# The pairs of the second mixer: 64x64 block products on all four quadrants of TensorE, in two token layouts

## The reference, cut to what matters

```python
def step(state, inp):
    r_t, w_t, k_t, v_t, kk_t, a_t = inp
    s_kk = jnp.einsum('bhij,bhj->bhi', state, kk_t)
    state = (state * w_t[:, :, None, :]
             - s_kk[..., None] * (kk_t * a_t)[:, :, None, :]
             + v_t[..., None] * k_t[:, :, None, :])
    return state, jnp.einsum('bhij,bhj->bhi', state, r_t)
```

## Time and profile before

| | us |
|---|---|
| median of 3 runs | 2676.55 |
| lowest and highest of the 3 | 2674.39, 2678.38 |
| span of the profiled execution | 2685.8 |
| PE busy in it | 2553.3 (95%) |
| DVE busy | 1283.3 (48%) |
| ACT busy | 678.3 (25%) |

### The profile page before, as it was taken

The page is one execution under the profiler, slowest core; times in us unless marked ns, Lnnn a source line. Parts: engine busy times, 40 slices in busy tenths (PEclk is TensorE's granted clock), DMA queues, the critical chain, the costliest instruction groups (busy, mean ns, idle before and its releaser), DMA issues. The chain is left out here.

```text
span 2685.8 us, 44310 instructions
## 1 busy us (share of the span) xinstructions
PE 2553.3 (95%) x17988; PEld 1728.1 (64%) x17988; DVE 1283.3 (48%) x2682; ACT 678.3 (25%) x1184; POOL 166.2 (6%) x128
## 2 busy tenths in 40 slices
PE   8999999999999899899998979999999999999997
PEld 3666666588875667566665636756787555677644
DVE  4656655667643222222222137524777335655525
ACT  2333333101112111111111111133454223343422
POOL 0000000000000022222222200000000000000000
PEclk9999999999999899999999989999999799999999
DMA  6222202335332789999999952441010232111120
GB/s 273 111 84 89 79 32 86 118 126 204 141 122 99 284 322 368 391 338 391 338 391 357 361 201 80 139 173 61 27 51 31 74 147 73 63 63 49 62 75 32
DMA packets 83737, 436.67 MB, mean 163 GB/s; under 512 B 16432, under 2 KB 16944, under 8 KB 39888
## 3 DMA queue, kind: packets, MB, share of 16 engines
q1 hardware_dynamic: 54592, 372.92, 35.3%
q0 software_dynamic: 18096, 37.80, 5.4%
q10 hardware_dynamic: 10848, 23.10, 2.3%
HBM read 400.65 MB, written 61.41 MB: 172 GB/s over the span
## 5 line engine op out<-in xcount | busy, mean ns | idle before, releaser
L284 PE MATMUL psum_all<-u,weights 128*128 128x512 f32 x704 | 306.9, 593 | 0.0
L284 PEld LDWEIGHTS psum_all<-u,weights 128*128 128x128 f32 x704 | 132.4, 190 | 157.7 <-issue 157.3
L964 PE MATMUL psum_all<-big,weights 128*128 128x256 f32 x928 | 214.7, 381 | 2.1 <-ACT sq L1021 1.3
L1898 PE MATMUL psum_all<-big 128*32 128x256 f32 (+2 forms) x1648 | 194.1, 382 | 8.1 <-DMA big<-t_experts 6.6
L1898 PE MATMUL psum_all<-weights,big 128*64 128x256 f32 (+2 forms) x1296 | 187.8, 388 | 10.2 <-DMA weights<-t_experts 9.5
L964 PEld LDWEIGHTS psum_all<-big,weights 128*128 128x128 f32 x928 | 174.5, 190 | 34.2 <-issue 5.1
L964 PE MATMUL psum_all<-big 128*128 128x256 f32 x784 | 179.0, 379 | 0.0
L1898 PEld LDWEIGHTS psum_all<-weights,big 128*64 128x64 f32 (+2 forms) x1296 | 131.9, 145 | 50.7 <-issue 16.1
L964 PEld LDWEIGHTS psum_all<-big 128*128 128x128 f32 x784 | 148.7, 190 | 22.4 <-DVE big L2617 0.8
L1898 PEld LDWEIGHTS psum_all<-big 128*32 128x32 f32 (+2 forms) x1648 | 136.0, 132 | 41.6 <-issue 10.0
L1933 DVE COPY big<-psum_all 128x256 f32<-128x256 f32 x46 | 19.5, 424 | 282.0 <-PE psum_all L294 282.0
(11 more groups left out here) (472 smaller groups left out, 3989.6 us busy)
## 6 DMA issues: line engine op xcount, KB each, us to landing
big<-t_experts SPq DMA_DIRECT2D x96, 1024.0 KB, 28.6
weights<-t_experts SPq DMA_DIRECT2D x96, 1024.0 KB, 26.7
weights<-t_ada SPq DMA_DIRECT2D x24, 1024.0 KB, 7.0
weights<-t_rkvg SPq DMA_DIRECT2D x16, 1024.0 KB, 8.6
rwkv_inputs<-big ACTq DMA_DIRECT2D x48, 256.0 KB, 2.3
big<-rwkv_inputs SPq DMA_DIRECT2D x8, 1280.0 KB, 6.8
weights<-t_x SPq DMA_DIRECT2D x8, 1024.0 KB, 4.8
weights<-t_BC SPq DMA_DIRECT2D x8, 1024.0 KB, 5.0
```

The lines of the kernel that those rows point to most:

```text
L284: last = pe.matmul(out, lhsT, rhs, start=n == 0, stop=n == len(terms) - 1)
L964: ins = pe.matmul(out, w[:, k, :], x[:, k, :], start=first and k == 0, stop=k == n - 1, skip_group_check=not first)
L1898: ins = pe.matmul(K.psum[rows, bank, n * F_E:(n + 1) * F_E], xT[:, k, rows], X.part(r, n, KD, F_E)[:, k, :], start=k == 0, stop=k == KD - 1)
```

## The change

Blocks get a new order, and there are two layouts of the tokens. `place(c, layout)` says for chunk c which partition half, which of two slots and which u it has; in layout 1 half and slot are exchanged. A set made by `turned_pe` reads one layout and writes the other: operands from half r, result in half `slot`, bank r of a unit. A unit is two banks (`K.unit` waits for the readers of both). Three sets (X0, X1, X2), each added to X on VectorE, go: the first inverse is now a product of A1, A2, A4 and A8, which are M and its powers with the identity added: P = A4·A1, Q = A2·P, X = A8·Q. P, Q and X are copied by ScalarE. Q alone stays in its layout (`straight_pe`, two quadrants).

```diff
-def blocks_pe(K, q, p, name, lhsT, rhs, reader):
-    for i in range(8):
-        for r in range(2):
-            ins = pe.matmul(K.psum[half(r), b, HEAD * i:HEAD * (i + 1)], lhsT[half(r), i, :], rhs[half(r), i, :],
+def place(c, layout):
+    u, tile_bit, half_bit = c // 4, c // 2 % 2, c % 2
+    return (tile_bit, half_bit, u) if layout == 0 else (half_bit, tile_bit, u)
+
+def turned_pe(K, q, p, name, lhsT, rhs, reader):
+    pe = K.nc.tensor
+    K.unit(UNIT[name], reader, name + " read", p)
+    for u in range(2):
+        for h in range(2):
+            for slot, r in ((0, 0), (1, 1), (1, 0), (0, 1)):
+                i = block(slot, u, h)
+                ins = pe.matmul(in_unit(K, name, half(slot), r, u, h), lhsT[half(r), i, :], rhs[half(r), i, :], start=True, stop=True)
+    ins.then_inc(*q.pe.tick(name, p))
@@ inside_pe: the same order of quadrants, first all four of qb, then all four of qk
@@ C1_pe: each of the 16 products of 64x128 becomes two of 64x64, one per layout
@@ turn_y_pe: 4 transposes become 4 matmuls by the identity
-    transposes(K, [(tile(K.psum[:, 7, :], t), X.yt[p % 2]...) for t in range(NT)])
+            ins = K.nc.tensor.matmul(out[:, u, slot], rows[:, slot, P * u:P * u + P], ident, start=True, stop=True)
@@ Q_pe, X_pe
+    K.nc.tensor.wait_ge(*q.dve.at("A2", p))
+    K.nc.tensor.wait_ge(*q.act.at("P read", p))
+    straight_pe(K, q, p, "Q", X.A2, X.N, q.act)
...
+    K.nc.tensor.wait_ge(*q.dve.at("NT3 read", p))
+    K.nc.tensor.wait_ge(*q.act.at("Q read", p))
+    turned_pe(K, q, p, "X", X.A8, X.NT, q.act)
@@ pair_pe: tv after to_state 1, bonus after to_state 2, NT, N, MT2 one place later
+    P_pe(K, X, q, s)
+    from_state_pe(K, X, q, s - 1, 6)
     NT3_pe(K, X, q, s)
-    from_state_pe(K, X, q, s - 1, 6)
-    tal_pe(K, X, q, s)
     to_state_pe(K, X, q, s - 1, 6)
     early.pe(s == KD, 1)
     tka_pe(K, X, q, s)
+    Q_pe(K, X, q, s)
     from_state_pe(K, X, q, s - 1, 7)
-    X2_pe(K, X, q, s)
+    X_pe(K, X, q, s)
@@ pair_act
+    P_act(K, X, q, s - 1)
     gain_act(K, X, q, s - 3)
     tka_act(K, X, q, s - 1)
     expp_act(K, X, q, s)
+    Q_act(K, X, q, s - 1)
+    X_act(K, X, q, s - 1)
     T16_act(K, X, q, s - 1)
@@ pair_dve: A2 for X0's add, A4 for X1's, A8 (two instructions) for X2's
     ends_dve(K, X, q, s - 1)
+    A4_dve(K, X, q, s - 1)
     S_dve(K, X, q, s - 2, 6)
-    add_X_dve(K, X, q, s - 1, "X1")
...
     normed_dve(K, X, q, s - 3)
+    A8_dve(K, X, q, s - 1)
     start_S_dve(K, X, q, s - 1)
-    add_X_dve(K, X, q, s - 1, "X2")
@@ al_dve and rh_dve: one 128x512 product becomes two of 128x256
+    for u in range(2):
+        ins = K.nc.vector.tensor_tensor(turned_chunks(X.alrh[p % 2], u, part_of), chunks(a, u), chunks(b, u), ALU.mult)
```

More of the change, by code:

```diff
@@ L267, in bank, with unit @@
         return self.psum[:, b, :]
+    def unit(self, n, signal, *key):
+        before = dict.fromkeys(self.held[b] for b in (2 * n, 2 * n + 1))
+        for earlier in before:
+            if earlier is not None:
+                s, k = earlier
+                self.nc.tensor.wait_ge(*s.at(*k))
+        self.held[2 * n] = self.held[2 * n + 1] = signal, key
 def load(K, i, view):
@@ L2719 @@
 SLOW = float(np.exp(-0.5))
[L2722 to L2726, removed]
+UNIT = {"y": 2, "T16": 0, "G16": 1, "A16": 1, "G32": 0, "T32": 1, "A32": 0, "TaT": 1, "Wv": 0, "C2": 1, "C1": 0, "MT": 1,
+        "WX": 0, "NT": 1, "N": 0, "MT2": 1, "M2": 0, "P": 1, "NT3": 0, "Q": 1, "X": 0}
+TOKENS_BANK = {"tv": 7, "tka": 7, "tal": 7, "tbe": 0}
 def outside(p):
@@ L2769, in channels_pe @@
[L2769 to L2777, removed]
-    ins.then_inc(*q.pe.tick(name, p))
+    half_of, slot, u = place(c, 0)
+    return X.alrh[p % 2][:, 2 * u + slot, :, HEAD * half_of:HEAD * (half_of + 1)]
@@ new lines, in straight_pe, with quarters @@
+def straight_pe(K, q, p, name, lhsT, rhs, reader):
+    pe = K.nc.tensor
+    K.unit(UNIT[name], reader, name + " read", p)
+    for slot in range(2):
+        for u in range(2):
+            for h in range(2):
+                i = block(slot, u, h)
+                for r in range(2):
+                    ins = pe.matmul(in_unit(K, name, half(r), slot, u, h), lhsT[half(r), i, :], rhs[half(r), i, :], start=True, stop=True)
+    ins.then_inc(*q.pe.tick(name, p))
+def quarters(layout):
+    for u in range(2):
+        for slot in range(2):
+            for r, h in ((0, 0), (1, 1), (0, 1), (1, 0)):
+                yield (4 * u + 2 * r + slot if layout == 0 else 4 * u + 2 * slot + r), h
@@ L2805, in tal_pe @@
     K.nc.tensor.wait_ge(*q.dve.at("al", p))
[L2806 to L2809, removed]
+    tokens_pe(K, q, p, "tal", lambda t: X.alrh[p % 2][:, t, 0, :])
 def C1_pe(K, X, q, p):
@@ L2983, in from_state_pe @@
         return
-    pe, rows = K.nc.tensor, half(c % 2)
+    pe, at = K.nc.tensor, P * (c % 2)
     if c == 0:
@@ L3038, in turn_y_pe @@
     K.bank(7, q.act, "yf", p)
-    transposes(K, [(tile(K.psum[:, 7, :], t), X.yt[p % 2].rearrange("p b n -> p (b n)")[:, t * P:(t + 1) * P]) for t in range(NT)]) \
-        .then_inc(*q.pe.tick("turn y", p))
+    rows = two_slots(X.yt[p % 2])
+    out = K.psum[:, 7, :].rearrange("p (u t r n) -> p u r t n", t=2, r=2, n=HEAD)
+    ident = K.c("ident").rearrange("p (t n) -> p t n", n=HEAD)
+    for u in range(2):
+        for slot in range(2):
+            ins = K.nc.tensor.matmul(out[:, u, slot], rows[:, slot, P * u:P * u + P], ident, start=True, stop=True)
+    ins.then_inc(*q.pe.tick("turn y", p))
 def mean_pe(K, X, q, p):
```

343 lines of the change are left out of this document (213 added, 130 removed).

## The result

The changed kernel takes 2729.15 us (median of 4 runs, 2724.57 to 2732.57) against 2675.47 us for the kernel before beside it (2673.17 to 2678.38): a ratio of 1.0189, with a 95% interval of 1.0162 to 1.0216. It is 53.7 us slower. The prediction, 2700.0 with a range of 2680 to 2722, has the direction and less than half of the size, and the measured time lies outside its range. The profiled execution has a span of 2725.7 us.

A forecast was written before the change was run, and what follows sets the result against it. VectorE was taken to bound the walk, a TensorE chain the tail. Per iteration -2.64 + 3.85 + 1.3 = +2.5, +2.3 with stalls, +4.1 with clock, times 6; with small terms +23.5, median 2676.55 to 2700, range 2680 to 2722.

The forecast's parts named there:

- the wait ahead of X: TensorE between from_state 7 and X: waiting for Q's copy behind gain, tka and Ep, 3.85 us more an iteration.
- the tail: From X to A32's adding: shorter sets on four quadrants, 10.74 us instead of 13.38, 2.64 less an iteration.
- the clock forecast at +1.8: TensorE right behind X: clock falls to 1.2 GHz at most waits, 1.8 us an iteration, from 0 to 2.6.
- the walk: Walk over the chunks: Al in halves, A4 and P, and Q ahead of from_state 7 add 1.3 us an iteration.
- I let half of it stay: Pairs' iterations: half the excess from stalls no engine's wait explains (mean 34.3 against 33.77) stays, making +2.5 into +2.3.
- the profile's 0.35% as a scale factor: Whole kernel: profiled execution lies 0.35% over the runs' median, so forecast 2709 for the profile becomes 2700 for the median.
- the last y gains about 1: Last y of the stage: about 1 us less.
- the first pairs: Pair 0: +1 us for one more level of product and copy; pair 1: -0.5 us, as X waits for A8 only.
- C: Rival: all as forecast, but the clock holds, +2.3 us in each of six iterations, 2690 us; chance 0.22.
- D: Rival: clock stays at 1.2 GHz for much of each iteration, some 8 us more each, 2725 us; chance 0.10.
- 21 us of work: TensorE in one iteration: claimed to work some 21 of 36 us, becoming 42 at 1.2 GHz.
- A: Rival: TensorE's work is what counts, 7.5 us less an iteration in full, 2617 us, or 2669; chance 0.12.

The follow-up runs named there:

- e5: Changed kernel with A4, A8, P and Q made earlier and gain behind X's copy on ScalarE: 2700.05 us, ratio 1.0085.
- e2: Changed kernel with four full-array matmuls that nothing reads filling TensorE's wait ahead of X: 2722.42 us, ratio 1.0151.
- e1: Kernel before, unedited, run and profiled once more: 2678.34 us, ratio 1.0001.
- e3: Changed kernel with one line moved, gain behind X's copy on ScalarE instead of ahead of tka's: 2718.22 us, ratio 1.0148.
- e10: Kernel of e5 with each turned set issuing 4 larger products instead of 16, output not the reference's: 2679.84 us, ratio 0.9999.
- e6: Changed kernel with matmuls that nothing reads ahead of X, P, TaT and to_state 0, in the last walk too: 2710.77 us, ratio 1.0138.
- e9: Changed kernel with each turned set issuing 4 larger products instead of 16, output not the reference's: 2719.22 us, ratio 1.0155.
- e7: Kernel before with two matmuls that nothing reads, ahead of TaT and to_state 0, in the last walk alone: 2676.79 us, ratio 1.0004.
- e8: Kernel of e5 with the two last-walk filling matmuls of e7 added: 2693.97 us, ratio 1.007.

## Why the prediction was off

**Right: the wait ahead of X.** 3.85 more was forecast, 4.13 behind from_state 7; measured are 4.32 in most iterations, 4.30 in the mean and 4.02 more than before, in the order gain, tka, Ep, Q. With the order that avoids it the kernel is 27 us faster by the excess (e5).

**Right: the tail.** 10.74 from X to A32's adding at full clock: 10.87 in the iteration of after that leads to pair 1, and in e2. With the clock forecast at +1.8, the tail's net is -0.84; measured is 12.85 against 13.81, -0.96. The page rule of the Trainium skill that was weighed there, in "TensorE: Matmul & The Clock Gate", section "Wait — 56ns, not 53.3ns?", an interval of at least about 25 ns from start to start, does not hold for these records: 32 of them start within 0.51 us in after as well (2097.39 to 2097.90 in its timeline), 16 ns each.

**Right at full clock, wrong as a whole: the walk.** The step is "I take 1.3 more, with bounds -0.5 and +2". The undisturbed walk takes 21.33 (1896.00 in after, one in e2), which is 1.3 over the 20.0 of before. Whether by the parts that were added up isn't shown: e5 takes Q out of the walk's end but puts A8 in. The mean is 23.35, 3.3 over e1 (3.18 over the first profile), beyond the bound. Two terms that the walk's sum did not have fill the gap:
- The clock in the walk. The prediction let it fall behind the wait of X alone and priced 5 us of it there. Measured are 25.8 us at 1.2 GHz in the six walks together. The two worst walks (8.8 and 10.2 us of it) took 25.31 and 26.31, 4 to 5 us over the undisturbed one, and the six together lost about 8.5 us by it, an estimate, 1.4 an iteration. The earlier trace rows had shown, at 2106, that the clock falls in a walk with small groups and waits between, without a long gap. The prediction read it and used it for a rival only.
- The gaps of instruction supply. "I let half of it stay" was the step: fewer stalls of the kind of the earlier trace rows were to come. (That one too stands 1.3 us behind a packet's end; the profile names ScalarE's copy, which had ended 0.8 us before it.) The reverse is so. They rose from 2.2 or 3.4 us to 6.0 from 1896 to 2139, and in the six walks from 1.3 or 0.8 to 4.9, some 0.6 a walk. The more of the waits is removed or filled, the more of them appears: 8.7 in e3, 9.5 in e2, 17.4 in e5.

The sum, 1.3 + 1.4 + 0.6 = 3.3, is the walk's excess. The split between the two last terms is read from single walks and is rough.

**Wrong: the profile's 0.35% as a scale factor.** The profiled execution lay 9 us over the median, and the prediction carried that over as if it were spread evenly, from 2709 to 2700. It was one place: the last walk at 0.66, 12 us. With it went the last term, "the last y gains about 1": the forecast let this stretch gain 1 us, and in the changed kernel's profile, where it is slow too, the rest is 12.5 longer than in e1. This is the largest single miss. The kernel before pays it in some of its runs and, by their times, in none of the four beside the changed kernel. What was to be read was the clock row of the page and the earlier trace rows, whose third line is in that walk. This is the clock row of the first profile:

```profile
PEclk9999999999999899999999989999999799999999
```

Slice 32, from 2081.5 to 2148.6 us, is its only dip from the stage of the pairs on.

**The sum of the misses.** Against e1 the forecast missed 6 x 2.04 = 12.2 in the walks (23.35 - 20.01 - 1.3), 13.5 in the rest (12.5 measured, -1 forecast) and 2.7 in the first pairs (3.2 measured, 0.5 forecast). Another 1.1 is the wait and the tail of the six iterations (37.9 measured, 24.6 forecast, less the 12.2). With the 23.5 of the forecast that is 53.0, against 53.6 between the spans and 53.7 between the medians. What makes up the 3.2 of the first pairs is not known.

**The rivals.** C (the clock holds) is out by the windows. D (the clock down much of each iteration, 2725, given 0.10) came nearest in time, with the wrong size at the wrong place: the clock is down for 64.9 us of the 243 of the six iterations, not in most of each. (No row gives its "21 us of work"; the profile has TensorE busy 29.33 us of 39.54 in the iteration from 1896.00.) Of A, the thought that TensorE's work counts, e10 shows the limit: even with the wait gone and the gaps gone, the tail at 11.15 and the wait at 0.63, an undisturbed iteration is 33.14 against 34.2: of the 2.75 that the tail gives (13.90 to 11.15), 1.3 goes back to the walk and 0.35 to the wait. In the mean e10's six iterations are 3.1 us shorter than e1's, and its time still equals that of the kernel before, for in its profile the rest is 9.2 longer, with the slow last walk.

**Open.** Why the clock falls in some walks and not in others of the same kernel. Some of it goes with the gaps: in the seven walks ahead of the last one, the kernels of the changed order have six gaps of 1.64 us or more together, and behind each the clock fell within 2.3 us; behind shorter ones (1.07 to 1.54) it fell so soon in three of 13 cases. Other falls have no such gap ahead of them. It fell in walks with the wait ahead of X filled (e2), with the other waits filled too (e6), without that wait (e5), and with larger products (e9); in e10, with no wait and few instructions, least (3.4 us in each of two walks). No kernel of the changed order kept it up in all pairs; the kernel before did, in its first profile (1.00 from 1836.00 to 2099.80). Open too is a form of the sets that computes the same by fewer instructions; it was not tried. No version run here beats the kernel before.

## What to carry to other kernels

A set that gets shorter pays only where its chain sets the end, and here the chain that fed it (gain, tka, Ep, Q in one engine's queue) cost more than the sets gave: place the last copy ahead of a critical product before anything that waits for another engine. When a profile lies above the median, find the place of the difference in the granted clock before scaling by it, and read each stretch in the profile in which the clock is down as a price that the same kind of stretch can pay anywhere. Small products packed on four quadrants raise the rate at which TensorE uses up instructions (32 records in 0.51 us, not in 0.98), so look at its idle time put down to "issue" before removing the waits that now cover it.

## What was not expected of the hardware

- **TensorE can run dry of instructions.** With 16 ns from record to record in straight-line code, gaps of up to 2.3 us stood inside and between sets, 17 of them in 243 us (e5); with 16 products of a set replaced by 4 of the same total time, one was left (e10). The Trainium skill says in "Runtime: NRT & Kernel Launch", section "Instruction fetch mechanics", that fetching is hidden because dispatch is slower than the refill. In these sets it isn't hidden: all 98 such gaps of the twelve profiles end 1.21 to 1.58 us behind the end of a 16 KB packet on the queue of instructions, and these packets fall from 45 to 27 where the gaps go (e10). The kernel before has such gaps too (seven, 2.2 us).
- **The clock falls without a long gap.** From 2017.78 to 2044.09, a walk with 20.35 of 26.31 us busy ran at 0.81, and the longest idle time in front of any of its matmuls was 1.77 us, against the 3.70 ahead of X. Ahead of the first fall, which came 0.1 us behind this gap, TensorE had been busy 4.92 of 8.51 us.
- **A last walk of one stage has two lengths.** 574.1 or 586.0 us from the last A32's adding to the end for one and the same program, with the granted clock at 1.00 or 0.66 over its first 40 us; with idle-filling matmuls in the walk it was 573.9 (e7), 574.9 (e6) and 577.4 (e8, the clock 0.96 over the first 40 us). But e9 has 572.6 without them, so one profile each doesn't show that they did it.
